# The opening of a two-block transformer kernel: adaptive weights loaded first, and their product with c split between TensorE and VectorE

## The reference, cut to what matters

```python
shift, scale, gate = jnp.split(c @ w_ada + b_ada, 3, axis=-1)
u = x * (1.0 + scale[:, None, :]) + shift[:, None, :]
h = split_cols(u @ w_in)       # queries, keys, values, gates of three mixers
...                            # three kinds of attention, mixed and gated
return layer_norm(ALPHA * x + (1.0 + gate[:, None, :]) * y, ln_g, ln_b)
```

## Time and profile before

| | us |
|---|---|
| median of 3 runs | 2393.32 |
| the three runs | 2391.03, 2393.32, 2450.62 |
| the profiled execution, its own time | 2391.5 |
| its span | 2389.7 |

### The profile page before, as it was taken

The page is one execution under the profiler, slowest core; times in us unless marked ns, Lnnn a source line. Parts: engine busy times, 40 slices in busy tenths (PEclk is TensorE's granted clock), DMA queues, the critical chain, the costliest instruction groups (busy, mean ns, idle before and its releaser), DMA issues.

```text
span 2389.7 us, 27225 instructions
## 1 busy us (share of the span) xinstructions
PE 2186.4 (91%) x10330; PEld 1726.4 (72%) x10330; DVE 1460.6 (61%) x1734; ACT 984.5 (41%) x1067; POOL 346.2 (14%) x234
## 2 busy tenths in 40 slices
PE   3999989999896879998778799999999999999997
PEld 3684656856584849987575687878788787878786
DVE  4224642145457533303963797878797897879786
ACT  0111511012112324431131575757666775757573
POOL 0000500000053237871720000000000000000000
PEclk9887788977897989998989899999999999999998
DMA  8253332432053026544400498989899898989894
GB/s 318 71 180 121 114 119 71 160 141 71 22 183 98 1 71 194 176 159 162 141 1 18 176 372 304 370 302 374 333 341 373 303 369 303 369 316 371 306 371 159
DMA packets 238542, 502.07 MB, mean 210 GB/s; under 512 B 11242, under 2 KB 52866, under 8 KB 238338
## 3 DMA queue, kind: packets, MB, share of 16 engines
q1 hardware_dynamic: 238466, 501.03, 58.7%
HBM read 499.96 MB, written 1.05 MB: 210 GB/s over the span
## 4 chain that ended last, share of the span: by engine, by line
PE 81%; DVE 12%; POOL 3%; ACT 2%; issue 1%; DMA 1%; SPq 0%; DVEq 0%; ACTq 0%; POOLq 0%
PE bank L1304 13%; PE bank L1289 9%; PE bank L1291 9%; PE bank L1290 9%; PE bank L700 6%; PE bank L888 5%; DVE cacc L2018 4%; PE bank L1007 3%; POOL ring_r L1686 3%; PE bank L1032 2%; PE bank L1183 2%; PE bank L839 2%; PE bank L987 2%; PE bank L707 2%; DVE qkv L2037 2%; PE bank L1213 2%
## 5 line engine op out<-in xcount | busy, mean ns | idle before, releaser
L2251 DVE TENSOR_TENSOR ring_r<-ring,more_his 128x2048 fp32r<-128x2048 f32 x192 | 433.5, 2285 | 10.6 <-ACT more_his L1334 10.4
L1334 ACT ACTIVATE more_his<-ring 128x2048 fp32r<-128x2048 f32 x192 | 359.0, 1908 | 13.5 <-DMA ring<-in_moe_w_down_dram 13.4
L1290 PE MATMUL bank<-ring_r,xe_hi 128*128 128x512 f32 x896 | 353.4, 394 | 0.0
L2251 DVE TENSOR_TENSOR ring_r<-ring,ring_r 128x2048 fp32r<-128x2048 f32 x144 | 325.2, 2286 | 24.9 <-ACT ring_r L1334 24.7
L1334 ACT ACTIVATE ring_r<-ring 128x2048 fp32r<-128x2048 f32 x144 | 268.0, 1907 | 3.8 <-DVE items L2218 3.8
L1289 PE MATMUL bank<-more_his,xe_hi 128*128 128x512 f32 x512 | 201.6, 394 | 0.0
L1291 PE MATMUL bank<-more_his,xe_lo 128*128 128x512 f32 x512 | 199.6, 390 | 0.0
L1290 PEld LDWEIGHTS bank<-ring_r,xe_hi 128*128 128x128 f32 x896 | 171.2, 191 | 34.7
L1304 PE MATMUL bank<-ring_r,he_hi 128*128 128x512 f32 x640 | 182.5, 391 | 0.0
L1289 PE MATMUL bank<-ring_r,xe_hi 128*128 128x512 f32 x384 | 156.7, 408 | 23.1 <-DVE ring_r L2251 23.1
L1686 POOL TENSOR_TENSOR ring_r<-ring,ff_hi 128x2048 fp32r<-128x2048 f32 (+1 forms) x34 | 156.9, 4640 | 91.1 <-ACT ff_hi L1334 91.1
(11 more groups left out here) (407 smaller groups left out, 3653.6 us busy)
## 6 DMA issues: line engine op xcount, KB each, us to landing
ring<-in_moe_w_gate_dram SPq DMA_DIRECT2D x112, 1024.0 KB, 5.2
ring<-in_moe_w_up_dram SPq DMA_DIRECT2D x112, 1024.0 KB, 5.3
ring<-in_moe_w_down_dram SPq DMA_DIRECT2D x112, 1024.0 KB, 4.9
ring<-in_w_in_dram SPq DMA_DIRECT2D x16, 2048.0 KB, 8.2
ring<-in_w_ada_dram SPq DMA_DIRECT2D x12, 2048.0 KB, 8.1
ring<-in_w_out_dram SPq DMA_DIRECT2D x8, 2048.0 KB, 7.8
ring<-in_w_in_dram SPq DMA_DIRECT2D x10, 1536.0 KB, 6.7
ring<-in_ffn_w_gate_dram SPq DMA_DIRECT2D x11, 1024.0 KB, 5.4
```

The source lines that it names most:

```text
L1290: mm(b[:, :], xe_hi[:, k, :], lo[:, kk, :], start=False, stop=False)
L1334: return go(out, in_, ACT.Copy, scale=scale)
L2251: tt(piece_lo(p), piece_raw(p), piece_hi(p).bitcast(fp32), ALU.subtract).then_inc(S("lo_ready"), 1)
```

## The change

- **Loads.** Ahead of ada0 stand only the rows and the first 384 columns of const (identity, causal mask, ones), with a semaphore of their own. x is issued behind ada1. perow, w2, b_f and the rest of const are issued behind the first part of w_in; const2 and router_w behind gate1.
- **The product with c in layer 0.** VectorE sums only chunks 0 to 3 of a group (ADA_DVE = 4). TensorE multiplies chunks 4 to 7 by c: c's column is stationary (one column), the chunk moves (512 columns), all into one partition of a bank; a fifth product, with ones stationary and VectorE's sum moving, completes the row (ada_row). ScalarE copies the row to SBUF (one partition, 512 numbers, kept in mix). Four products of one row each, with a moving operand of one number, put it onto the partitions (ada_column, new jobs adaT0 to adaT3 in bank 5). VectorE adds the bias as before.
- **Order.** TensorE: row 0, row 1, column 0, turn x, row 2, column 1, row 3, column 2, column 3. VectorE: the four steps of a group, then the bias addition of the group before.
- **perow** is turned between the projections (job pe, bank 3), and copied by ScalarE there.
- Waits for const and for the small loads stand further back on each engine. Layer 1 keeps its way.

```diff
+NFIRST = CONST_AT["ones"][1]
+ADA_DVE = 4
@@ plan_first
-            add(f"ada{q}", [7, 4, 5, 6][q])
+            add(f"ada{q}", [7, 4][q % 2])
+            add(f"adaT{q}", 5)
...
+    if l == 0:
+        add("pe", 3)
@@ sync
-            sp.dma_start(const[:, :], A["const"]).then_inc(S("const_loaded"), 16)
-            sp.dma_start(perow[:, :], ...)
-            sp.dma_start(w2[:, :, :, :], ...)
-                sp.dma_start(b_f[:, :], ...)
-            sp.dma_start(const2[:, :], ...)
-            sp.dma_start(router_w[:, :, :], ...)
-            sp.dma_start(x[:, :, :], ...)
+            sp.dma_start(const[:, 0:NFIRST], A["const"][:, 0:NFIRST]).then_inc(S("ident_loaded"), 16)
             for n, (name, k, width, src) in enumerate(loads):
...
+                if name == (0, "ada1"):
+                    sp.dma_start(x[:, :, :], ...)
+                if name == (0, W_IN_PARTS[0][0]):
+                    # perow, w2, b_f, then:
+                    sp.dma_start(const[:, NFIRST:], A["const"][:, NFIRST:]).then_inc(S("const_loaded"), 16)
+                if name == (0, "gate1"):
+                    # const2, router_w
@@ tensor
+            def ada_row(q):
+                j = jobs[0, f"ada{q}"]
+                b = take(pe, j)
+                w = weights(pe, (0, f"ada{q}"))
+                for k in range(ADA_DVE, KD):
+                    mm(b[0:1, :], vecs[:, k:k + 1], w[:, k, :], start=(k == ADA_DVE), stop=False)
+                pe.wait_ge(S("ada_summed"), q + 1)
+                done(mm(b[0:1, :], C("ones")[:, 0:1], w[:, 0, :], start=False, stop=True), j)
+
+            def ada_column(q):
+                copied(pe, jobs[0, f"ada{q}"])
+                j = jobs[0, f"adaT{q}"]
+                b = take(pe, j)
+                for m in range(4):
+                    last = mm(b[:, 4 * q + m:4 * q + m + 1], ada_rows(q)[:, m * P:(m + 1) * P], C("ones", 1)[:, 0:1],
+                              start=True, stop=True)
+                done(last, j)
...
             for q in range(4):
-                shift_scale(0, q)
+                if q == 2:
+                    turn_x(0)
+                ada_row(q)
+                if q:
+                    ada_column(q - 1)
+            ada_column(3)
@@ scalar
+            for q in range(4):
+                j = jobs[0, f"ada{q}"]
+                free(copy(ada_rows(q), filled(act, j)[0:1, :]), j)
@@ vector
             for q in range(4):
-                for k in range(KD):
-                    ada_step(0, q, k)
-            for q in range(4):
-                shift_scale(0, q)
+                for k in range(ADA_DVE):
+                    ada_step(0, q, k, ADA_DVE)
+                if q:
+                    shift_scale(0, q - 1)
+            shift_scale(0, 3)
```

More of the change, by code:

```diff
@@ L178, with shift_scale_of @@
 GATE_BY, NEXT_FROM, NEXT_BY = 7, 4, 16
+ADA_DVE = 4
+def shift_scale_of(l, q):
+    return l, f"adaT{q}" if l == 0 else f"ada{q}"
 MIX_COL = {"dsa": 0, "fox": 256, "cmp": 640, "win": 640, "slc": 640}
@@ L574, in piece_hi, with ada_rows @@
             return half_slot(ring_r, MOE_RING + p % MOE_RING, p)
+        def ada_rows(q):
+            return mix[0:1, q // 2, q % 2 * 512:(q % 2 + 1) * 512]
         def copied(eng, job):
@@ L634, in _ @@
                     sp.dma_start(dst[:, :, q * w:(q + 1) * w], piece).then_inc(slot_loaded[s], 16)
+                if name == (0, "ada1"):
+                    sp.dma_start(x[:, :, :], A["x"][0].rearrange("(i p) d -> p i d", p=P)).then_inc(S("x_loaded"), 16)
+                if name == (0, W_IN_PARTS[0][0]):
+                    sp.dma_start(perow[:, :], A["cmp_pe"].rearrange("l v i d -> (l v i) d")).then_inc(S("small_loaded"), 16)
+                    sp.dma_start(w2[:, :, :, :], A["cmp_w2"].rearrange("l v a b -> a l v b")).then_inc(S("small_loaded"), 16)
+                    with nc.allow_non_contiguous_dma(reason="12 numbers"):
+                        sp.dma_start(b_f[:, :], A["b_f"].rearrange("l h -> h l")).then_inc(S("small_loaded"), 16)
+                    sp.dma_start(const[:, NFIRST:], A["const"][:, NFIRST:]).then_inc(S("const_loaded"), 16)
+                if name == (0, "gate1"):
+                    sp.dma_start(const2[:, :], A["const2"]).then_inc(S("const2_loaded"), 16)
+                    sp.dma_start(router_w[:, :, :], A["router_w_2"][0].rearrange("(k p) e -> p k e", p=P)).then_inc(S("router_loaded"), 16)
                 if name[-1] == "nsa_vs":
@@ L727, in rotate @@
                 done(mm(b[0:r, 0:tiles * T], C(f"rot{dim}", r)[:, 0:r], raw[name][0:r, :, :], start=True, stop=True), j)
-            pe.wait_ge(S("const_loaded"), 16)
+            pe.wait_ge(S("ident_loaded"), 16)
             pe.wait_ge(S("rows_loaded"), 48)
             nc.tensor.transpose(bank[6][:, 0:40], rows[0:40, :], C("ident", 40)[:, 0:40]).then_inc(S("vecs_T"), 1)
-            pe.wait_ge(S("small_loaded"), 48)
-            nc.tensor.transpose(bank[5][0:HD, 0:P], perow[:, :], C("ident")).then_inc(S("pe_T"), 1)
             pe.wait_ge(S("vecs_ready"), 1)
-            pe.wait_ge(S("pe_ready"), 2)
+            def ada_row(q):
[14 more added lines that the diff above has]
+                done(last, j)
             def shift_scale(l, q):
@@ L740, in shift_scale @@
                 b = take(pe, j)
-                pe.wait_ge(S("ada_summed" if l == 0 else "ada_next"), q + 1)
+                pe.wait_ge(S("ada_next"), q + 1)
                 w = weights(pe, (l, f"ada{q}"))
@@ L745, in shift_scale, with turn_x @@
                 done(last, j)
-            for q in range(4):
-                shift_scale(0, q)
-            for l in range(DEPTH):
+            def turn_x(l):
                 if l == 0:
@@ L762, in _ @@
                     done(last, j)
+            for q in range(4):
[5 more added lines that the diff above has]
+            ada_column(3)
+            for l in range(DEPTH):
+                if l:
+                    turn_x(l)
                 for m in range(4):
@@ L773, in _ @@
                 feats(l, "dq", ("dsa_q", 0, P), ("dsa_q", P, P))
+                if l == 0:
+                    pe.wait_ge(S("small_loaded"), 48)
+                    j = jobs[0, "pe"]
+                    done(nc.tensor.transpose(take(pe, j)[0:HD, 0:P], perow[:, :], C("ident")), j)
+                    pe.wait_ge(S("const_loaded"), 16)
                 rotate(l, "iq")
@@ L1340, in norm_scale @@
                     go(lnmv[:, i, 2:3], lnmv[:, i, 1:2], ACT.Sqrt).then_inc(S("std_ready"), 1)
-            act.wait_ge(S("pe_T"), 1)
-            for v in range(2):
-                go(pe_sb[v * HD:(v + 1) * HD, :, :, :], bank[5][0:HD, 0:P], ACT.Copy).then_inc(S("pe_ready"), 1)
+            for q in range(4):
+                j = jobs[0, f"ada{q}"]
+                free(copy(ada_rows(q), filled(act, j)[0:1, :]), j)
             for l in range(DEPTH):
                 for q in range(4):
-                    copied(act, jobs[l, f"ada{q}"])
+                    copied(act, jobs[shift_scale_of(l, q)])
                 for m in (1, 3):
@@ L1362, in _ @@
                 free(copy(raw["dq"][:, :, :], filled(act, j)[:, :], HD ** -0.5), j)
+                if l == 0:
+                    j = jobs[0, "pe"]
+                    b = filled(act, j)
+                    copy(pe_sb[0:HD, :, :, :], b[0:HD, 0:P])
+                    free(copy(pe_sb[HD:P, :, :, :], b[0:HD, 0:P]), j)
                 j = jobs[l, "dkv"]
@@ L1749, in residual @@
                     norm(q, i, z)
-            dve.wait_ge(S("const_loaded"), 16)
             dve.wait_ge(S("vecs_T"), 1)
@@ L1754, in _, with ada_step @@
             dve.wait_ge(S("vecs_ready"), 1)
-            dve.wait_ge(S("pe_ready"), 2)
-            dve.wait_ge(S("small_loaded"), 48)
             def shift_scale(l, q):
-                j = jobs[l, f"ada{q}"]
+                j = jobs[shift_scale_of(l, q)]
                 b = filled(dve, j)
                 part = slice(4 * q, 4 * q + 4)
-                free(stt(adac[:, part], b[:, 0:4], 0.0 if q < 2 else 1.0, vec_bada(l)[:, part], ALU.add, ALU.add), j)
-            def ada_step(l, q, k):
+                at = 4 * q if l == 0 else 0
+                free(stt(adac[:, part], b[:, at:at + 4], 0.0 if q < 2 else 1.0, vec_bada(l)[:, part], ALU.add, ALU.add), j)
+            def ada_step(l, q, k, upto=KD):
                 w = weights(dve, (l, f"ada{q}"))
@@ L1771, in ada_step @@
                 ins = stt(w[:, 0, :], w[:, k, :], vec_c(k), w[:, 0, :], ALU.mult, ALU.add)
-                if k < KD - 1:
+                if k < upto - 1:
                     link(ins)
@@ L1777, in _ @@
             for q in range(4):
-                for k in range(KD):
-                    ada_step(0, q, k)
-            for q in range(4):
-                shift_scale(0, q)
+                for k in range(ADA_DVE):
[3 more added lines that the diff above has]
+            shift_scale(0, 3)
             for l in range(DEPTH):
                 for q in range(4):
-                    copied(dve, jobs[l, f"ada{q}"])
```

(7 more changed lines are left out.)

## The result

| | median us | executions |
|---|---|---|
| before | 2394.36 | 4: 2391.03 to 2450.62 |
| changed | 2430.11 | 4: 2428.49 to 2444.66 |

The account below looks back on a forecast made before the run. TensorE lies on 81% of the chain of waits, but the opening is bound by the first weights' transfer, then VectorE's steps. First projection 8.5 us sooner, perow's turning taking some back: net -8.2, 2391.5 to 2383.3 us; range 2377 to 2397.

Parts of the forecast that it names:

- Loads: Opening: 2.85 MB go from ahead of the first weights, 7.9 us, so these land at 11.3 us instead of 19.2.
- The row products: Opening, TensorE: five per group, 4.3 us at 2.4 GHz or 8.6 at 1.2; they lift the clock like projections.
- Rival B: Opening: the row products never lift the clock, each group takes 8.6 us; 2400.3 us in total, chance 0.14.
- The slow side for the turning of x: Opening: 16 transposes at 1.2 GHz, 3.5 us, and group 2 6.0; if they kept a high clock, 3.4 us sooner.
- The sum for the undisturbed run: Whole kernel: opening 8.5 us less, perow's turning a little back, net -8.2, so 2391.5 becomes 2383.3 us.
- Behind it, every later stage only starts earlier ... I take a third of it as scatter either way.: After the opening: 10 us at half clock in the fox stage cost up to 5 us, a third taken as scatter.
- Rival C: Attention stages stay at half clock up to 10 us longer, 4 us per layer, 8 together: 2390 to 2392, chance 0.10.
- The third run of before: Whole kernel: one of three earlier runs was 2.4% above the others; within 2% 0.95, faster 0.02, slower 0.03.
- Edits at no cost: const2 and router_w moved behind gate1, costed at nothing; perow's turning adds one transpose, 0.22 us, to twice that.

Follow-up runs that it names:

- e1: The changed kernel again, no edit: thirteen executions, six at 2382.0 to 2386.9 us, five at 2428 to 2433, two at 2444; ratio 0.9962.
- e10: The kernel before with only perow's turning moved, between the dsa_q projection and the first rotation; lowest 2393.6 us, three of twelve above 2420.
- e12: The changed kernel with x turned after the last column products; lowest 2382.4 us, five of twelve above 2420.
- e5: The changed kernel with VectorE summing all eight chunks (no shared product), x still turned early; lowest level 2381.9 to 2382.7 us, six of twelve above 2420.
- e8: The changed kernel plus unread dense products: three at step 7 of both attention stages, two at step 14, one at 16 in layer 0; median 2384.44 us.
- e4: The changed kernel plus unread dense products in each attention stage: four at step 1, among the fox scores, three at step 7; median 2388.8 us.

## Why the prediction was wrong, point by point

- **Loads.** First weights used at 10.6 us, forecast 11.3. Right; and no later wait of TensorE on a load in the changed kernel's profile.
- **The row products.** Price, the rise of the clock, and 2.4 GHz from group 1: right. The rise came later than in the sum: group 0 took 7.3 us, forecast 6.0. Rival B (2400, no rise) didn't occur: its number was nearest to the result for a wrong reason.
- **The slow side for the turning of x.** Wrong: 1.90 us, at 2.4 GHz, and group 2 fast at once. Turning and group took 6.3 us instead of 9.5, 3.2 too dear. Group 0 took 1.3 of that back, and what follows the last row product another 1.0 (5.2 us instead of 4.2: the last column products started 1.3 us after it, not 0.7, and took 1.17, not 0.84). First projection 40.06, forecast 41.4: part of the opening's closeness is errors that cancel.
- **The sum for the undisturbed run.** -8.2 forecast; in e1 the lowest executions are 2382.0 against 2389.1, -7.1, and the median of the six low ones against that of the nineteen low ones of before 2382.3 against 2390.8, -8.5. Right.
- **"Behind it, every later stage only starts earlier ... I take a third of it as scatter either way."** This is the step that failed. I had seen 60 and 50 us at 1.2 GHz for the same work and read it as a spread of 10 us. The runs say that it was the sign of a stage on an edge: what can vary is not how late the clock is raised but whether it is raised at all, and that costs 33 and 35 us, not 4. Rival C named the place and the mechanism, and priced it at 8 us for both layers; it measured 67.6. Its size was to be had from the profile of before: 41 us of the first stage and 44 of the second ran at 2.4 GHz (271.7 to 312.6, 565.2 to 609.6), and at 1.2 GHz the same pair of records starts 1.15 us after the last (261.53 and 262.68 in the changed kernel) instead of 0.63, which makes 34 and 37 us more. What the runs don't show is why the changed opening meets that edge more often.
- **The third run of before,** 2450.62, I took for a stray value and used for a chance alone. It was the kernel's own third level, in 14 of 116 executions.
- **Edits at no cost.** The perow turning was priced 0.2 to 0.4 us; e10's lowest is up by 5.8. Whether that is work or a shift of the clock isn't separated.

## What to carry to other kernels

Where the timing runs scatter by more than a stage can explain, look at the granted clock stage by stage before pricing any change ahead of that stage: a stage that works without a pause and still stays at 1.2 GHz for part of its length is an edge, as far as these profiles show, and a shift of tenths of a microsecond may decide over its whole remainder. Price "never raised" as a case of its own, and consider a few dense products that nobody reads at the start of the part that can hold the clock. Test each half of a combined change alone: here the order of the loads, with the early turning of x, carried the gain, and the shared product almost none.

## What the runs showed of the hardware that I had not expected

Transposes can raise TensorE's clock. The clean case is e12: the clock fell as the turning of x began, nothing but its 16 records ran from 36.3 to 39.9, at 1.2 GHz (3.62 us), and then the clock was up (windows):

```profile
37.00:39.00 2.00, 2.00 (x11) 0.50 1.06 373
40.00:56.00 16.00, 14.67 (x82) 1.00 0.77 271
```

The first projection behind it took 10.71 us for 48 records, where the kernel before needed 12.36 after the same turning: there it began at 1.2 GHz, so the turning doesn't raise the clock every time. In e5 the sixteen transposes of x began at 24.3 us at 1.2 GHz, right behind column products; the next column products, at 29.98, took 1.05 us, where those ahead of the transposes took 1.87, and the fall was recorded only after 31.7 (timeline, then windows):

```profile
22.57 1.87 PE L780 MATMUL bank<-const,ring 128*128 128x1 f32 x8 [4.02 <-DVE ring L1818]
24.30 3.65 PE L794 MATMUL bank<-const,x 128*128 128x128 f32 x16
29.98 1.05 PE L780 MATMUL bank<-const,ring 128*128 128x1 f32 x8 [2.03 <-DVE ring L1818]
35.89 1.86 PE L780 MATMUL bank<-const,ring 128*128 128x1 f32 x8 [4.86 <-DVE ring L1818]
```

```profile
28.00:31.00 3.00, 1.02 (x8) 1.00 1.06 368
32.00:36.00 4.00, 0.11 (x1) 0.50 1.05 375
```

The Trainium skill ("TensorE: Matmul & The Clock Gate", Part 4) says that transposes don't count as busy for the clock; for these f32 transposes the measurement says otherwise, and it decides. Products with a single stationary column raise it too (6.48 us for the first group's four, 3.43 for the next). And the same work can run at either level for a long time: the later part of layer 0's attention stage held 2.4 GHz from 271.7 to 312.6 in the kernel before, while in the changed kernel it was issued without a pause and stayed at 0.50 to the end of the stage. The earlier part, where scores that use 64 or six of the 128 rows stand among products that use all, stayed at 0.50 for 51 us in e8 (200.2 to 251.3), and lost a clock that a burst had raised (e4). What tells work that keeps the clock from work that raises it, the runs don't show.
